# Fourteen modulation chunks of a two-layer diffusion step are moved beside one top-k

## What is computed

```
sh1, sc1, g1, sh2, sc2, g2 = adaln(cond, mod_w, mod_b)        # silu(cond) @ mod_w + mod_b, 1024 x 6144
mix, ... = token_mixers(modulate(x, norm1_w, sh1, sc1), ...)  # pooling, state-space scan, attention
x = x + g1 * mix
x = x + g2 * peer_ffn(modulate(x, norm2_w, sh2, sc2), lp)
```

## Time and profile before

| | us |
|---|---|
| median of 3 executions | 2899.43 (2888.21 to 2899.82) |
| the profiled execution, its own time | 2908.34 |
| its span | 2906.4 |
| PE busy in it | 1603.9 |
| DVE busy in it | 1573.3 |
| POOL busy in it | 1458.8 |
| bytes moved | 969.34 MB, mean 334 GB/s |

### The profile page before, as it was taken

How to read it: one execution, slowest core, us unless ns; L and a number is a source line. 1 busy time by engine, 2 the same in 40 slices (tenths; PEclk the granted TensorE clock), 3 DMA queues, 4 the chain that set the end, 5 groups by cost and what they waited for, 6 DMA issues and landing times.

```text
span 2906.4 us, 20766 instructions
## 1 busy us (share of the span) xinstructions
PE 1603.9 (55%) x6712; PEld 700.7 (24%) x6712; DVE 1573.3 (54%) x4174; ACT 263.0 (9%) x587; POOL 1458.8 (50%) x1540
## 2 busy tenths in 40 slices
PE   6777835866424555673347784687520154453455
PEld 2344522353001221251011353245100010010011
DVE  1327884555878445547820667272769455445500
ACT  1311122101000010100000022110000000000000
POOL 0000544444665655455666524442555666667664
PEclk8879867878656776776569886887755576675577
DMA  7544977887999999999999777785897999999997
GB/s 299 229 167 184 398 298 271 333 317 264 351 368 411 414 413 390 415 383 375 369 382 373 308 313 298 270 334 215 313 348 282 380 365 369 370 365 390 363 366 290
DMA packets 238045, 969.34 MB, mean 334 GB/s; under 512 B 26314, under 2 KB 28746, under 8 KB 227954
## 3 DMA queue, kind: packets, MB, share of 16 engines
q0 software_dynamic: 221184, 805.40, 72.4%
q1 hardware_dynamic: 16754, 162.61, 14.0%
HBM read 964.77 MB, written 3.15 MB: 333 GB/s over the span
## 4 chain that ended last, share of the span: by engine, by line
PE 32%; DVE 21%; issue 19%; POOL 12%; DMA 10%; another core or an unknown queue 4%; ACT 2%; SPq 0%; DVEq 0%; ACTq 0%
PE acc L923 11%; PE psum L879 7%; DVE rows L1644 5%; POOL work L601 5%; POOL rows L601 5%; PE psum L680 4%; DMA work<-peer_v_in,vidx 3%; DMA rows<-peer_v_in,vidx 3%; PE psum L868 2%; DVE work L1644 2%; DMA work<-peer_u_in,idx 2%; POOL wring L601 2%; PE psum L640 2%; DVE work L1252 2%
## 5 line engine op out<-in xcount | busy, mean ns | idle before, releaser
L601 POOL DMA_INDIRECT rows<-peer_u_in,idx x496 | 468.7, 945 | 652.1 <-DVE idx L1337 281.6
L1644 DVE CUSTOM_DVE_ANT_0 rows<-rows,h_kept 128x1024 f32<-128x1024 f32 x496 | 582.4, 1217 | 166.3 <-DMA rows<-peer_u_in,idx 130.8
L601 POOL DMA_INDIRECT rows<-peer_v_in,vidx x454 | 436.3, 961 | 404.1 <-PE acc L923 201.5
L923 PE MATMUL acc<-rows,vw 128*32 128x512 f32 x1664 | 368.4, 831 | 367.2 <-DMA rows<-peer_v_in,vidx 191.2
L923 PE MATMUL acc<-work,vw 128*32 128x512 f32 x736 | 221.4, 825 | 305.7 <-issue 200.7
L1644 DVE CUSTOM_DVE_ANT_0 work<-work,h_kept 128x1024 f32<-128x1024 f32 x208 | 247.9, 1218 | 163.3 <-DMA work<-peer_u_in,idx 139.5
L601 POOL DMA_INDIRECT work<-peer_v_in,vidx x242 | 228.8, 945 | 175.0 <-issue 62.9
L601 POOL DMA_INDIRECT work<-peer_u_in,idx x208 | 196.2, 943 | 124.3 <-issue 52.5
L879 PE MATMUL psum<-work,wring 128*128 128x256 f32 (+1 forms) x960 | 192.4, 360 | 65.0 <-issue 62.3
L923 PEld LDWEIGHTS acc<-rows,vw 128*32 128x32 f32 x1664 | 74.2, 135 | 589.6 <-issue 562.2
L680 PE MATMUL psum<-wring,work 128*128 128x512 f32 (+1 forms) x464 | 182.9, 548 | 14.3 <-issue 10.7
(11 more groups left out here) (218 smaller groups left out, 1851.4 us busy)
## 6 DMA issues: line engine op xcount, KB each, us to landing
wring<-mod_w_in SPq DMA_DIRECT2D x21, 2048.0 KB
wring<-w_in_in SPq DMA_DIRECT2D x18, 2048.0 KB
wring<-peer_wq_in SPq DMA_DIRECT2D x15, 2048.0 KB
wring<-w_out_in SPq DMA_DIRECT2D x7, 2048.0 KB
rows<-peer_u_in,idx POOLq DMA_INDIRECT x496
rows<-peer_v_in,vidx POOLq DMA_INDIRECT x454
work<-mod_w_in SPq DMA_DIRECT2D x3, 2048.0 KB, 7.5
wring<-w_in_in SPq DMA_DIRECT2D x4, 1056.0 KB
```

What stands on the lines that cost most here:

```text
L601: nc.gpsimd.indirect_dma_start(slots[slot_of[n]], None, table, bass.IndirectOffsetOnAxis(ap=at[:, col + r:col + r + 1], axis=0))\
L923: ins = mm(acc[half][QUAD * j:QUAD * (j + 1), :], w[:, at:at + QUAD], four[j][0][:, half * CHUNK:(half + 1) * CHUNK], start=(r == 0), stop ...
L1644: V.tensor_tensor_reduce(held, held, h_kept[:, :], 1.0, 0.0, ALU.mult, ALU.add, dots[:, dots_at(k, t) + r:dots_at(k, t) + r + 1]).then_inc ...
```

## The change

The last two chunks of layer 0 and all twelve of layer 1 are loaded and summed beside the top-k of step 1: (0,10) at `("ps", 0)`, (0,11) and (1,2), (1,3), (1,0), (1,1) at the first five pauses of the first tile, the other eight of layer 1 at the eight pauses of the second. DVE takes them one pause later than PE and ACT. They use another place for `mod_part`. Step 2 has no modulation of its own, and its pauses lose the four `mod` entries (weights 238.5 in all); steps 0 and 2 have no "late" part. PE computes the key scores of step 1's second tile only behind the first tile's fifth pause. In `chunks` and in SP's program the fourteen chunks stand behind the query weights of step 1.

```diff
+MOD_BESIDE = dict(zip((("ps", 0), *(("choose", 0, i) for i in range(5)), *(("choose", 1, i) for i in range(8))),
+                      [(0, 10), (0, 11)] + [(1, j) for j in MOD_ORDER]))
...
-        mod_part = region(17456, CHUNK)
+        mod_parts = {True: region(17456, CHUNK), False: region(8216, CHUNK)}
+
+        def mod_part(layer, j):
+            return mod_parts[(layer, j) not in MOD_BESIDE.values()]
...
-            if st.first:
-                chunks += [(("mod", st.layer, j), ("mod", st.layer, j)) for j in MOD_ORDER[10:]]
+            if k == 1:
+                chunks += [(("mod", *which), ("mod", *which)) for which in MOD_BESIDE.values()]
...
-                if st.first:
-                    modulation(layer, MOD_ORDER[10:])
+                if k == 1:
+                    for which in MOD_BESIDE.values():
+                        load_chunk("mod", *which)
...
             def widen_first(st):
-                pe.wait_ge(*after("mod_whole", st.layer, 0))
+                if st.layer:
+                    pe.wait_ge(*taken("modr", st.layer, MOD_ORDER[-1]))
+                pe.wait_ge(*after("mod_whole", st.layer, st.layer))
...
+            def modulate_beside(st, point):
+                if st.k == 1 and point in MOD_BESIDE:
+                    layer, j = MOD_BESIDE[point]
+                    for _ in modulation(layer, (j,)):
                         pass
...
+                key_scores(0)
+                if T == 2 and not st.early:
+                    key_scores(1)
                 for t in range(T):
                     yield ("ps", t)
+                    modulate_beside(st, ("ps", t))
                     for i in range(8):
                         yield ("choose", t, i)
+                        modulate_beside(st, ("choose", t, i))
+                        if st.early and (t, i) == (0, 4):
+                            key_scores(1)
                     yield ("exp", t)
-                modulate_at(st, "late")
...
-                if layer and not n:
-
-                    act.wait_ge(*after("picked", 2 * layer - 1, steps[2 * layer - 1].T - 1))
...
+            points = [("ps", 0), *(("choose", 0, i) for i in range(8)), *(("choose", 1, i) for i in range(8)), ("exp", 1)]
+
+            def modulate_beside(st, point):
+                if st.k == 1 and point in points[1:]:
+                    behind = points[points.index(point) - 1]
+                    if behind in MOD_BESIDE:
+                        take_rows(*MOD_BESIDE[behind])
...
-    if st.first and st.k:
-        names += [(("mod", j), 8) for j in MOD_ORDER[:4]]
```

More of the change, by code:

```diff
@@ L372, in build_pass @@
             k, last = st.k, st.T - 1
-            if st.first:
-                chunks += [(("mod", st.layer, j), ("mod", st.layer, j)) for j in MOD_ORDER[:4]]
+            if k == 0:
+                chunks += [(("mod", 0, j), ("mod", 0, j)) for j in MOD_ORDER[:4]]
             if not st.early:
@@ L378, in build_pass @@
                        (("xb1", k), ("xb", k, 5)), (("xb0", k), ("xb", k, 3)), (("pz", k), ("pz", k, last))]
-            if st.first:
-                chunks += [(("mod", st.layer, j), ("mod", st.layer, j)) for j in MOD_ORDER[4:10]]
+            if k == 0:
+                chunks += [(("mod", 0, j), ("mod", 0, j)) for j in MOD_ORDER[4:10]]
             chunks += [(("wo", k, cc), ("wo", k, last, cc)) for cc in range(2)]
@@ L504, in _ @@
                 if st.first:
-                    modulation(layer, MOD_ORDER[2 if k == 0 else 0:4])
+                    if k == 0:
+                        modulation(0, MOD_ORDER[2:4])
                     load_chunk("q", k)
@@ L544, in _ @@
                       .then_inc(*mark("newv", layer, n=16))
-                    modulation(layer, MOD_ORDER[4:10])
+                    if k == 0:
+                        modulation(0, MOD_ORDER[4:10])
                 load_chunk("wo", k, 0)
@@ L631, in add_groups @@
                 pe.wait_ge(*taken("mod", layer, j))
-                mm(p[of_layer(layer), :], c("rows_of", 22 - 2 * j, 24), mod_part, start=True, stop=True)\
+                mm(p[of_layer(layer), :], c("rows_of", 22 - 2 * j, 24), mod_part(layer, j), start=True, stop=True)\
                     .then_inc(*made("modr", layer, j))
@@ L654, in modulate_at @@
             def modulate_at(st, point):
-                if st.first:
-                    for _ in modulation(st.layer, MOD_AT[point]):
+                if st.k == 0:
+                    for _ in modulation(0, MOD_AT[point]):
+                        pass
+            def modulate_beside(st, point):
+                if st.k == 1 and point in MOD_BESIDE:
+                    layer, j = MOD_BESIDE[point]
+                    for _ in modulation(layer, (j,)):
                         pass
@@ L885, in dense, with key_scores @@
                 pe.wait_ge(*after("keys_in", k))
-                for t in range(T):
+                def key_scores(t):
                     for i in range(4):
@@ L939, in take_rows @@
                     act.wait_ge(*full("modr", *((layer, MOD_ORDER[n - 1]) if n else (layer - 1, MOD_ORDER[-1]))))
-                if layer and not n:
-                    act.wait_ge(*after("picked", 2 * layer - 1, steps[2 * layer - 1].T - 1))
                 act.wait_ge(*full("mod", layer, j))
-                A(mod_part, bank("mod", layer, j)[:, :], ACT.Copy).then_inc(*take("mod", layer, j))
+                A(mod_part(layer, j), bank("mod", layer, j)[:, :], ACT.Copy).then_inc(*take("mod", layer, j))
             def widen(st, vec, name, dst):
@@ L974, in modulate_at @@
             def modulate_at(st, point):
-                if st.first:
+                if st.k == 0:
                     for j in MOD_AT[point]:
-                        take_rows(st.layer, j)
+                        take_rows(0, j)
+            def modulate_beside(st, point):
+                if st.k == 1 and point in MOD_BESIDE:
+                    take_rows(*MOD_BESIDE[point])
             def carry(dst, src, *key, scale=1.0):
@@ L1610, in dense @@
                         yield ("ps", t)
-                    yield from choose(st, t)
-                modulate_at(st, "late")
+                    for name in choose(st, t):
+                        yield name
+                        modulate_beside(st, name)
             def share(k, t, q):
@@ L1837, in work @@
         ahead = opening(following) if following and following.early else None
[L1838 to L1841, removed]
+        if st.k == 0:
+            for _ in modulation(0):
+                pass
         if not st.early:
```

11 lines of the change are left out of this document (6 added, 5 removed).

## The result

The kernel after takes 2923.7 us (median of 8, 2920.3 to 2942.6), the kernel before beside it 2899.6 (8 runs): a ratio of 1.0096, 95% interval 1.007 to 1.0122. It is 24 us slower, by 28 if one takes the ratio. The forecast was 2881, the range ended at 2912.

What follows compares the result with a forecast made beforehand. The DMA engines were taken to bound step 2 (408 GB/s), with open DMA time in step 1's top-k. Terms 43 - 53 - 7 - 2 = -19 us took the median from 2899.4 to 2881 us; range 2862 to 2912.

Steps and rivals of the forecast that it cites:

- term B: Step 2 with its tail, 828 to 1620 us: loses 21.0 MB of chunks, keeps 392 GB/s, -53 us.
- this case: Sign of a wrong forecast: step 2 with its tail, relieved of chunks, slows because DVE or PE sets its pace; unpriced.
- A: Top-k of step 1, 677 to 828 us: gets 25.2 MB of chunks, runs at 385 GB/s, +43 us.
- spread of 13 gather events: Step 2: gathers from the four modulation pauses spread over other pauses, bytes moved anyway; no cost.
- step 0's late pair: Step 0: no late chunk pair, so DVE starts u rows 5.1 us earlier and chunks leave a full stretch; -7 us.
- step 2's late part: Step 2 behind its gates: the late sums, 4.6 us on DVE, go; -2 us (0 to 5).
- The sign named beforehand: Step 1's top-k: forecast wrong if DVE waits for modulation sums more than some 20 us in all.
- chunks set the pace: Rival: second tile of step 1 waits for a chunk each pause, +79 us with the first tile; 2916 us, chance 0.16.
- Bytes only change place: Rival: step 1's top-k runs at 359 GB/s, +57 us, sum -5; 2894 us, chance 0.27.

Runs made afterwards that it cites:

- e1: Kernel before with the ten second-layer modulation chunks that step 2 loads cut to 64 KB each, slower kind of chip: 2888.2 us, 0.9965 of before.
- e7: Kernel after with the rows gathered beside step 2 cut to a quarter, faster kind of chip: 2611.3 us, 0.9727 of before.
- h1: Kernel before with step 2's ten modulation chunks cut to 64 KB each, faster kind of chip: 2644.7 us, 0.9857 of before.
- e3: Kernel after with the second layer's twelve chunks cut to 64 KB each, slower kind of chip: 2891.1 us, 0.9978 of before.
- i2: Kernel before with the weight of step 2's four modulation pauses set to 0, slower kind of chip: 2929.5 us, 1.0037 of before.
- e2: Kernel after with four empty pauses of weight 8 put back ahead of step 2's opening, slower kind of chip: 2911.2 us, 1.0038 of before.
- i1: Kernel after with the four lost pauses' weights added to the first pauses of step 2's opening, slower kind of chip: 2924.4 us, 1.0034 of before.
- e4: Kernel before with only the first layer's late chunk pair moved beside step 1's top-k, plus late key scores, slower kind: 2892.2 us, 0.9978 of before.
- g4: Kernel of e4 plus the second layer's last two chunks at the first two pauses of step 2's top-k, faster kind: 2693.9 us, 1.0039 of before.
- h3: Kernel before with only the first layer's late chunk pair beside step 1's top-k, plus late key scores, faster kind: 2695.4 us, 1.0032 of before.
- g1: The kernel after, unchanged, measured again on the faster kind of chip: 2696.0 us, 1.004 of before.
- e6: Kernel before with the weight of step 2's four modulation pauses set to 0, faster kind of chip: 2683.9 us, 0.9988 of before.
- h4: Kernel after with only the second tile's eight second-layer chunks cut to 64 KB each, faster kind of chip: 2660.2 us, 0.9915 of before.
- e8: Kernel before with only step 1's second-tile key scores moved behind the first tile's fifth pause, faster kind of chip: 2685.2 us, 1.0001 of before.

## Why the prediction was wrong

The step that failed is term B: "Without 21.0 MB it moves 289.5, and at its own mean rate of 392 GB/s that takes 739 us". The bytes were right (287.0 MB by the trace after), the rate was not. 392 is a mean of 408 in the dense part, where eight of the ten chunks and the weights stood beside the gathers (plain loads are 22% of its bytes), and of 374 and 382 behind it, where plain loads are 12% and 7%. After the change B ran at 371, its dense part at 369. Taking out the chunks' bytes alone (e1) gave 10 us where 53 were forecast, and the dense part fell to 375 GB/s. The trace of before said so in step 3 (373 GB/s, and 215 to 390 GB/s in the last 14 slices of the earlier trace rows); I took the mean of the stretch with the filler for that of the stretch without it. "I keep the rate" leaned on the top-k of step 2 having room for more gathers: it got them (153 to 181 rows) and its rate went from 374 to 378 only. I had named this case among what would make the forecast wrong, with VectorE or TensorE as its cause, and gave it neither a price nor a chance. On the faster kind e7 and h1 show that neither engine is the bound by itself. On the slower kind the hole read under e1 is such a case: the chain of ScalarE, VectorE and TensorE stood, though none of them was busy.

The terms on the slower kind, each measured by itself as a ratio to before and times 2899:

| term | predicted | measured |
|---|---|---|
| A's bytes (after less e3) | +43 | +34 |
| B's bytes (e1) | -53 | -10 |
| spread of 13 gather events (i2; e2 and i1: 17 and 18) | 0 | +11 |
| step 0's late pair (predicted: step 0 alone; measured, e4: with its bytes in A) | -7 | -6 |
| step 2's late part (g4 against h3, faster kind) | -2 | not seen |
| sum | -19 | +29 |
| the change itself | | +28 |

The first row and the change share a run, so what the sum tests is the rest: -10, +11 and -6 make -5, and e3 by itself measured -6. Each measured term is uncertain by some 5 to 10 us, and i2 ran on another chip than e1 to e4, so that the sum agrees so closely is luck; that B and the spread carry the error is not.

Point by point:

- **A** was right on the slower kind, in length and rate; with the second layer's chunks light, at most 7 us of its growth stay for the coupling of the engines (e3). On the faster kind it cost 53, because the stretch around it moved 374 GB/s before and left less open, while B gave back 43. The sign named beforehand, VectorE waiting more than 20 us for modulation sums in A, is not reached in the trace after (15 us in all) and is reached in g1 (22 us). The 359 GB/s of the rivals was read from the last 149 us of step 2's top-k; the whole stage (1215 to 1471 us) reads 374.
- **The spread** was put at nothing, because these are "bytes that B moves anyway". True on the faster kind (e6: -3 us, within its interval). On the slower kind it costs 11 to 18 us: the top-k stage of step 2 then takes 280 to 288 us where it took 248, and the dense part gives back less. Why the slower kind gains only 20 us there was not tried.
- **Step 0** gave 3 us of the 7 in the profile after, 7 in that of e4. The two chunks leave a stretch with idle DMA engines (0.46), so they free no DMA time. That A gets 4.2 MB more than B loses stood in the prediction's bytes; on the faster kind, where nearly all stretches of steps 1 and 2 are full, this alone would account for the result: 4.2 MB at 409 GB/s are 10.3 us, g1 is 11 us slower, h3 9 to 11.
- **The rival "chunks set the pace"**, with 2916 the nearest, is not what happened in the second tile: A grew by 39 to 42 us (53 on the faster kind), below its 62, and h4 and the 1.3 us wait show no pace there. In the first tile, to which it gave 6 us, the chunks did hold VectorE (12.5 us after, 22 in g1). "Bytes only change place" comes near to the faster kind.
- **The step-2 late part** (-2): g4 against h3 shows nothing (1.0039 and 1.0032, on two chips).

Nothing tried beats the kernel before on both kinds of chip: e4 is 0.2% faster on one and 0.3% slower on the other.

## What to carry to other kernels

When a transfer is taken out of a stretch, price what is left by the rate of stretches that have no such transfer, not by the mean of the one that has it; a steady weight load beside gathers may be filling holes, and then its bytes are nearly free where they stand. Here that pricing would have served: the 289.5 MB left in B take 758 to 776 us at 382 to 373 GB/s (773 measured, the new spread included), and 708 us at the faster kind's 409 (710 measured). Bytes are also free where the engines are half idle: moving such a load into a full stretch, to shorten a wait of a few us, can cost its full time (h3), and in a stretch with room it did not (e4). And removing pauses moves the work that was laid on them: count per stage what the planner now puts where.

## What the runs showed of the hardware that was not expected

On one kind of chip this same kernel takes 7.4 to 8% less time than on the other (2685 against 2899 to 2917 us), at nearly the same granted clock (0.704 to 0.742 and 0.711 to 0.744 over the runs of before). Both move 408 to 413 GB/s when gathers and plain loads stand together. Gathers alone hold 409 GB/s over 150 us (2250 to 2400) on the faster and 373 on the slower (368 to 385 in its eight traces), with dips. Of the 226 us between the spans of the kernel before and of e8, 146 lie behind step 2 (1286 and 1140 us), where gathers are 94% of the bytes.

A packet's own time does not show it: a 4 KB packet of a gather takes 159 ns on the slower and 160 on the faster (medians over the traces of before and e8). What differs is how the engines get on. The page's chain that ended last, share of the span, before and then e8:

```profile
PE 32%; DVE 21%; issue 19%; POOL 12%; DMA 10%; another core or an unknown queue 4%; ACT 2%; SPq 0%; DVEq 0%; ACTq 0%
...
DMA 30%; PE 25%; DVE 22%; POOL 14%; issue 7%; ACT 2%; SPq 0%; POOLq 0%; DVEq 0%; ACTq 0%
```

"issue" is time in which an engine waited for nothing that the profile shows. It is 16 to 26% in the eight traces of the slower kind and 7% in each of the twelve of the faster, and "another core or an unknown queue" stands on the slower kind alone, with one core at work. A part of this may be missing records, but not all: VectorE reads a dot product's sum 1.14 to 1.15 us after the product's start, with nothing of the program between them, and on the slower kind 6 to 21 of the 768 reads come later, after 1.4 or 2.1 us, while on the faster none does. So engines that stand still have a part in the dips, as in the hole read under e1; how large a part was not measured. Why they stand still stays open.

The same edit changed its sign between the two (e4 and h3), and the worth of the same 20.3 MB went from 11 us to 40 (e1, h1): a result of half a per cent from one chip doesn't carry to another by itself.

The Trainium skill's HBM limit of about 358 GB/s for a core ("DMA: Bandwidth & Descriptors", section Specifications), which would also have forecast no gain, is not the reason for it: the same page, section Bandwidth, says that a core gets this when both cores of its HBM domain stream. This case's traces agree that it does not hold a single core: one core here moved 413 GB/s over 387 us (e8).
